# Query and key halves leave the projection stage, stacked scores of a differential attention, transposes between the score halves

## The reference

```python
def diff_attn_block(q1, q2, k1, k2, v, lam):
    scale = B_HEAD_DIM ** -0.5
    s1 = jnp.einsum('bhqd,bhkd->bhqk', q1, k1).astype(jnp.float32) * scale
    s2 = jnp.einsum('bhqd,bhkd->bhqk', q2, k2).astype(jnp.float32) * scale
    p = jax.nn.softmax(s1, axis=-1) - lam * jax.nn.softmax(s2, axis=-1)
    return jnp.einsum('bhqk,bhkd->bhqd', p.astype(v.dtype), v)
...
    p = h @ w_in                         # 2 x 512 columns for the convolution, 512 q, 512 k, 512 v
    qx = rope_2d(qx)                     # only the 1024 tokens are rotated, not the context
    kx = rope_2d(kx)
    u = a[..., :A_WIDTH] * jax.nn.sigmoid(a[..., A_WIDTH:])
    u = depthwise_conv(u, conv_w, conv_b)      # 31 taps
```

## Time and profile before

| | |
|---|---|
| median of 3 runs | 4222.05 us (4220.51 to 4226.47) |
| the profiled execution, its own time | 4207.65 us |
| its span (first to last instruction) | 4206.0 us |
| mean granted clock of TensorE | 0.92 |
| TensorE busy | 3500.0 us (83%) |
| VectorE busy | 2124.1 us (51%) |
| ScalarE busy | 1261.2 us (30%) |
| GpSimd busy | 223.8 us (5%) |

### The profile page before, as it was taken

How to read it: one execution, slowest core, us unless ns; L and a number is a source line. 1 busy time by engine, 2 the same in 40 slices (tenths; PEclk the granted TensorE clock), 3 DMA queues, 4 the chain that set the end, 5 groups by cost and what they waited for, 6 DMA issues and landing times. The chain is left out here.

```text
span 4206.0 us, 48006 instructions
## 1 busy us (share of the span) xinstructions
PE 3500.0 (83%) x18199; PEld 2870.6 (68%) x18199; DVE 2124.1 (51%) x2406; ACT 1261.2 (30%) x2015; POOL 223.8 (5%) x335
## 2 busy tenths in 40 slices
PE   2898677739799999999494888888888479999996
PEld 1776455527688888888393767667776468888884
DVE  4598354474434434444452565555556454444445
ACT  2111244353211112111242554444455222111121
POOL 0011000001100000000030000000000010000000
PEclk6899788879899999999696999999999789999998
DMA  4211433223211011100322000000000521111112
GB/s 158 68 60 62 165 136 133 91 90 120 61 40 50 30 35 35 50 30 21 136 87 76 14 12 12 12 12 4 13 5 6 185 81 47 47 56 40 50 50 90
DMA packets 233242, 259.87 MB, mean 62 GB/s; under 512 B 51424, under 2 KB 190400, under 8 KB 232112
## 3 DMA queue, kind: packets, MB, share of 16 engines
q1 hardware_dynamic: 226768, 241.02, 17.6%
q0 software_dynamic: 6368, 17.39, 1.3%
HBM read 217.42 MB, written 40.96 MB: 61 GB/s over the span
## 5 line engine op out<-in xcount | busy, mean ns | idle before, releaser
L1010 DVE TENSOR_TENSOR y_sum<-ffn_down_ps,y_sum 128x512 f32<-128x512 f32 x396 | 271.7, 690 | 253.1 <-PE ffn_down_ps L90 253.1
L88 PE MATMUL ffn_gate_ps<-y_hi,ffn_w_hi 128*128 128x512 f32 (+1 forms) x880 | 326.0, 370 | 31.8 <-DVE ffn_w_lo L971 31.8
L89 PE MATMUL ffn_gate_ps<-y_lo,ffn_w_hi 128*128 128x512 f32 (+1 forms) x880 | 325.5, 370 | 0.0
L90 PE MATMUL ffn_gate_ps<-y_hi,ffn_w_lo 128*128 128x512 f32 (+1 forms) x880 | 325.1, 369 | 0.0
L89 PE MATMUL ffn_val_ps<-y_lo,ffn_w_hi 128*128 128x512 f32 (+1 forms) x880 | 323.9, 368 | 0.0
L88 PE MATMUL ffn_val_ps<-y_hi,ffn_w_hi 128*128 128x512 f32 (+1 forms) x880 | 323.8, 368 | 0.0
L90 PE MATMUL ffn_val_ps<-y_hi,ffn_w_lo 128*128 128x512 f32 (+1 forms) x880 | 323.7, 368 | 0.0
L88 PE MATMUL ffn_down_ps<-ffn_w_hi,ffn_act_hi 128*128 128x512 f32 x792 | 312.1, 394 | 13.2 <-DVE y_sum L1010 6.8
L89 PE MATMUL ffn_down_ps<-ffn_w_lo,ffn_act_hi 128*128 128x512 f32 x792 | 309.6, 391 | 0.0
L90 PE MATMUL ffn_down_ps<-ffn_w_hi,ffn_act_lo 128*128 128x512 f32 x792 | 309.3, 390 | 0.0
L971 DVE TENSOR_TENSOR ffn_w_lo<-ffn_raw,ffn_w_hi 128x1024 fp32r<-128x1024 f32 x132 | 158.0, 1223 | 280.9 <-ACT ffn_w_hi L934 280.9
(11 more groups left out here) (270 smaller groups left out, 7764.6 us busy)
## 6 DMA issues: line engine op xcount, KB each, us to landing
ffn_raw<-in_ffn_w_up SPq DMA_DIRECT2D x88, 512.0 KB, 3.8
da_ada_w<-in_ada_w SPq DMA_DIRECT2D x10, 4096.0 KB, 13.0
ffn_raw<-in_ffn_w_down SPq DMA_DIRECT2D x44, 512.0 KB, 5.6
ab_raw<-in_ab_w_in SPq DMA_DIRECT2D x20, 512.0 KB, 3.7
scratch_x<-out_x SPq DMA_DIRECT2D x18, 512.0 KB, 2.6
mod_ada_w<-in_ada_w SPq DMA_DIRECT2D x4, 2048.0 KB, 11.1
scratch_qk<-ab_qk POOLq DMA_DIRECT2D x8, 640.0 KB, 3.3
da_raw<-scratch_qk SPq DMA_DIRECT2D x8, 640.0 KB, 4.7
```

Source lines behind the costliest of these rows:

```text
L88: pe.matmul(out, a_hi, b_hi, start=first, stop=False)
L89: pe.matmul(out, a_hi, b_lo, start=False, stop=False)
L90: return pe.matmul(out, a_lo, b_hi, start=False, stop=last)
L1010: dve.tensor_tensor(part, down_ps[:, half, :], part, ALU.add).then_inc(s.sum_done, 1)
```

## The change

Four things change.

1. In the projection stage GpSimd splits each finished q or k piece: a cast to fp32r (`qk_hi`), a subtraction (`qk_lo`), and two stores to two DRAM tensors.
2. The attention stage loads the parts. `q_stacked` holds on partitions 0 to 63 the hi part of q and on 64 to 127 the lo part, with the two score halves side by side in the free dimension; `k_hi` and `k_lo` are loaded twice, once on each half of the partitions. Six loads per head take the place of two, and no engine splits.
3. A score half is then two matmuls per chunk, stacked q by `k_hi` and stacked q by `k_lo`, over 128 rows each (with them the product lo by lo is computed as well). The first half's scores wait for the first exponential only, the second half's for the second.
4. The queues: TensorE puts the groups of transposes between the two halves' scores; products come one unit later; the modulation group moves to n % 4 == 2; VectorE runs combine(n) ahead of maxima(n+1).

```diff
@@ GpSimd, projection stage
                 for j in range(2):
                     n = i * 2 + j
                     pool.wait_ge(s.sum_done.sem, s.sum_done.nth(n))
-                    pool.dma_start(qk[n * P:(n + 1) * P, :], qk_t[:, j, :]).then_inc(qk_stored[j].sem, 16)
-                for j in range(2):
-                    pool.wait_ge(qk_stored[j].sem, qk_stored[j].nth(i))
-                    pool.sem_inc(s.qk_free.sem, 1)
+                    if i:
+                        pool.wait_ge(qk_stored[j].sem, qk_stored[j].nth(i - 1))
+                    pool.tensor_copy(qk_hi[:, j, :], qk_t[:, j, :]).then_inc(s.qk_hi_done.sem, 1)
+                    pool.wait_ge(s.qk_hi_done.sem, s.qk_hi_done.nth(n))
+                    if n:
+                        pool.wait_ge(qk_stored[1 - j].sem, qk_stored[1 - j].nth((n - 1) // 2))
+                    pool.tensor_tensor(qk_lo[:, :], qk_t[:, j, :], qk_hi[:, j, :].bitcast(F32), ALU.subtract)\
+                        .then_inc(s.qk_free.sem, 1)
+                    pool.dma_start(qk[0][n * P:(n + 1) * P, :], qk_hi[:, j, :].bitcast(F32)).then_inc(qk_stored[j].sem, 16)
+                    pool.wait_ge(s.qk_free.sem, s.qk_free.nth(n))
+                    pool.dma_start(qk[1][n * P:(n + 1) * P, :], qk_lo[:, :].bitcast(F32)).then_inc(qk_stored[j].sem, 16)
@@ SyncE, attention stage
+            def head(h):
+                j, rows = h % 2, B_HEADS * 2 * B_DIM
+                if h >= 2:
+                    sp.wait_ge(s.s2_full.sem, (h - 1) * NU)
+                def halves(part, first):
+                    return qk[part][first + h * 2 * B_DIM:first + (h + 1) * 2 * B_DIM, :]\
+                        .rearrange("(a d) t -> d a t", a=2)
+                for part in range(2):
+                    at = slice(part * B_DIM, (part + 1) * B_DIM)
+                    sp.dma_start(q_st[at, j, :, :].bitcast(F32), halves(part, 0)).then_inc(qk_in[j].sem, 16)
+                for k, part in ((k_hi, 0), (k_lo, 1)):
+                    for copy in range(2):
+                        sp.dma_start(k[copy * B_DIM:(copy + 1) * B_DIM, j, :, :].bitcast(F32), halves(part, rows))\
+                          .then_inc(qk_in[j].sem, 16)
@@ VectorE
-            for n in range(ALL + 2):
+            for n in range(ALL + QP + 1):
+                if n < ALL:
+                    combine(n)
                 if n + 1 < ALL:
                     maxima(n + 1)
-                if n % QP == 1 and n > QP:
-                    output(n // QP - 1)
+                if n and pair_at(n - 1) is not None:
+                    output(pair_at(n - 1))
                 if n and window(n - 1) is not None:
                     m.add(dve, window(n - 1))
-                if n < ALL:
-                    combine(n)
-                    if split_at(n):
-                        second_half(*split_at(n))
@@ TensorE
-            def scores(n):
+            def scores(n, half):
...
-                    for q, k in ((q_hi, k_hi), (q_lo, k_hi), (q_hi, k_lo)):
-                        for half, full in ((0, s.s1_full), (1, s.s2_full)):
-                            dims = slice(half * B_DIM, (half + 1) * B_DIM)
-                            mm = pe.matmul(s_ps[:, half, keys], q[dims, j, rows], k[dims, j, keys],
-                                           start=q is q_hi and k is k_hi, stop=k is k_lo)
-                            if k is k_lo and a + width == T:
-                                mm.then_inc(full.sem, 1)
+                    pe.matmul(s_ps[:, half, keys], q, k_hi[:, j, half, keys], start=True, stop=False)
+                    mm = pe.matmul(s_ps[:, half, keys], q, k_lo[:, j, half, keys], start=False, stop=True)
+                mm.then_inc(full.sem, 1)
...
-            for n in range(ALL + 1):
-                if n + 2 < ALL:
-                    scores(n + 2)
-                if n < ALL:
-                    turned(n)
-                if n % QP == 0 and n:
-                    product(n // QP - 1)
+            for n in range(ALL + QP):
+                for at in range(3):
+                    if n < ALL and at < len(groups(n)):
+                        turned(n, at)
+                    if n + 2 < ALL and at < 2:
+                        scores(n + 2, at)
+                if pair_at(n) is not None:
+                    product(pair_at(n))
                 if window(n) is not None:
```

More of the change, by code:

```diff
@@ L529, in project_conv_diff @@
         part = sb("part", [P, 2, SEQ])
+        qk_hi = sb("qk_hi", [P, 2, T], F32R)
+        qk_lo = sb("qk_lo", [P, T], F32R)
         v_t = sig
@@ L1186, in _ @@
             m.load(sp, 0)
-            piece(1, 0)
-            piece(1, 1)
+            head(1)
+            m.load(sp, 1)
             values(1)
-            m.load(sp, 1)
             m.load(sp, 2)
-            piece(2, 0)
-            piece(2, 1)
+            head(2)
             m.load(sp, 3)
@@ L1196, in _ @@
             m.load(sp, 4)
-            piece(3, 0)
-            piece(3, 1)
+            head(3)
             m.load(sp, 5)
```

97 lines of the change are left out of this document (39 added, 58 removed).

## The result

The changed kernel takes 4153.74 us (median of 4, 4149.86 to 4158.33). The kernel before took 4221.28 us beside it (median of 4, 4214.8 to 4226.47). The ratio is 0.9841, 95% interval 0.9824 to 0.9858: faster by 1.6%. The forecast was 4180 with a range of 4132 to 4214; the gain was forecast at 42 us and came out at 67.5.

A forecast was written before the change was run, and what follows sets the result against it. The prediction took attention to be bound by waits in a ring between engines and projection by VectorE. Attention -83, projection +36 and start +5 gave -42, from the median 4222.05 to 4180 us, range 4132 to 4214 (forecast's own case 4155 to 4205).

The forecast's parts named there:

- the rival without exclusion: Projection stage: GpSimd's casts and subtractions run beside VectorE's convolution, losing only 8 us; 4152 us, chance 0.12.
- Attention, -83 forecast: Attention stage: four heads of 66 us plus 8 for the start and 7.5 for the tail, 280 us, 83 less.
- my 7% on top of the walk: Attention heads: queue walk gave 62 us, raised to 66 because the old ring's walk fell some 7% short of the trace.
- The ring of 6.35 us: Attention, plain unit: combine, first maximum to first exponential, second exponential, and its becoming visible follow one another, about 6.35 us.
- a clock near 1: Attention stage: TensorE's longest idle gap falls from 4.04 to 2.5 us, so its granted clock rises from 0.84 to near 1.
- The splits explain about 40 us: Attention stage before: without splits a head costs about 77 us and the stage about 323, so splits explain 40 of 363.
- Projection, +36 forecast: Projection stage: GpSimd's operations cost 28.5 us in turns 1 to 3 and 7 for the last pieces; bounds 27 and 45.
- The exclusion: Projection stage: GpSimd and VectorE block each other, so each GpSimd cast (2.0 us) or subtraction (2.75) costs VectorE its whole length.
- Start, +5 forecast: Start of attention: 3.9 MB in six loads before the first scores; +0 at 410 GB/s, +9 at half rate, middle taken.
- The clock that stays low: Attention stage: TensorE's clock keeps 0.84, a head takes 74 us and the stage 311; 4211 us, chance 0.11.
- Only the splits' gain: Attention wins only the splits' 40 us and the projection stage gives them back; 4223 us, chance 0.07.
- The wait for the output: Attention: second transposes wait for VectorE's output, closing a ring of 9.7 us per product unit; at worst 4239 us, chance 0.08.

The follow-up runs named there:

- one_product: Changed kernel without the score matmuls with k's rest (q times k_lo left out); ratio 0.9827 to the kernel before, attention stage 258.1 us.
- split_moved_only: Kernel before with only the split moved to the projection stage, attention unstacked and in its old order, loading parts; 4222.56 us against 4217.85.
- The 2x2 table: Stacked kernels with TensorE's and VectorE's orders each old or changed; stage: both old 339.1, VectorE's changed 320.2, TensorE's changed 367.0, both 269.6 us.
- no_pool_split: Changed kernel without GpSimd's cast and subtraction of q and k in the projection stage, the unsplit sum stored twice; 4130.54 us.
- maxima_first: Changed kernel with VectorE doing maxima(n+1), output and the ada addition ahead of combine(n), as before; 4254.31 us.

## Why the prediction was right, and where it was off

**The sign and its cause** were right: attention wins far more than projection and start lose. At the end of attention the balance was -60.7, forecast -42. The number 4153.74 itself proves little: it lies just below the forecast's own 4155 to 4205 and beside the 4152 of the rival without exclusion, which the traces refute. Attention won 16.9 us more than forecast, projection lost 5.0 less and the start 3.3 more.

**Attention, -83 forecast, -99.9 measured.** Of the 16.9 us between them, 6.6 were a reading error: I took the output at 829.66 for the last, and the stage before was that much longer. The other 10 are in the stage after, 269.6 instead of 280. The heads came every 64.0, 64.6 and 65.2 us (first maxima at 508.55, 572.50, 637.08 and 702.30), the last with its tail took 73.2, against 66 and 73.5: my 7% on top of the walk was too much. The start took 2.6 us from first scores to first maxima, not the 8 that I allowed. The ring of 6.35 us a plain unit was right: five maxima in a row begin 6.36 us apart (515.18 to 540.62). So was a clock near 1 (0.98), but not its reason, the shorter gaps: in one_product TensorE's longest wait for an exponential was 2.3 us, about the 2.2 of the changed kernel, and its clock was 0.89.

**What carried it was put wrongly.** "The splits explain about 40 us" is a mis-sized term: moving them alone is worth 26.5. The misread output is in it as well. From the maxima at 745.32 to the true last output the fourth head takes 90.9 us, not 84.3; with my 7.5 for the tail a head without splits is then 83.4, the stage 349, and the splits explain some 20. In split_moved_only the heads take 85.1, 83.8 and 80.0 us, not 77. Against that, the order is worth 69.5 where the forecast left some 43 for it. I wrote that what the halves buy is the ring, with `combine` in it as an added 1.9 us. The 2x2 table shows that without `combine` in front TensorE's new queue buys nothing and costs 27.9, since its first transposes stand ahead of the scores and wait for `combine`. VectorE's moved lines were no price of the new order but its condition.

**Stacking** was priced at +18 us of TensorE's time, and the pitch of 0.23 us for a single matmul is as forecast (538.49 to 538.72). In the old order it cost the stage nothing (343.0 to 339.1): TensorE was busy for 273.4 us instead of 269.9, at a clock of 0.91 instead of 0.87. Its price came at the start: 12.1 us, of which the moved split gives 3.7 back. In one_product, in the new order, 39 us less of matmuls gave 11.5.

**Projection, +36 forecast, +31.0 measured.** The exclusion was right in kind: no_pool_split shows that the convolution's longer steps are GpSimd's doing. The cast was mis-sized, 1.25 to 1.40 us instead of 2.0. The subtraction takes 2.88 undisturbed; the forecast had worked out 2.9 and added up 2.75. That each operation costs VectorE its whole length was a little too much: two of each are 8.3 us, and a turn grew by 6.7. One of the two casts falls on the rotation, whose addition took 2.17 instead of 1.23, a loss of 0.9. So the three turns cost 22.0 us instead of 28.5 (the third store of the convolution went from 348.15 to 370.10), and the last pieces 9.0 instead of 7: the two errors partly cancel. GpSimd's subtraction did wait for the store before it, four times and 14.0 us in all, which the forecast put under the cast; what that costs was not separated.

**Start, +5 forecast, +8.3 measured.** I took the middle of two bounds, +0 and +9; the upper one, loads at half the rate, was right.

**Rivals.** No exclusion: refuted by the steps beside GpSimd. The clock that stays low: refuted at 0.98. Only the splits' gain: refuted by the 69.5 us of the order; split_moved_only, which has the splits' gain alone, comes out level as said. The wait for the output: it exists on VectorE (45.9 us) and ScalarE (26.9 us), but TensorE waits for no output ahead of its second transposes, and the ring of 9.7 us did not close. In maxima_first a ring of 10.5 us did, through product, output and `combine`.

## What to carry to other kernels

When two engines hand work back and forth, change both queues together and test each alone: half of a good reordering can be slower than none (367.0 against 339.1), and the whole much better than either. In a stage where an engine waits for another's last result, look for work that is already free to run and put it between the halves of the waiting operation. Work that is moved to an idle engine is not free if it takes the bound engine's access with it: GpSimd's casts and subtractions cost VectorE 6.7 us a turn, while its own subtractions cost 3.0.

## What the runs showed of the hardware

- GpSimd's cast f32 to fp32r over 128x1280 takes 1.25 us undisturbed, its subtraction 2.88, VectorE's 1.48. Three-operand convolution steps of VectorE (1.57 us) reach 4.26 us beside GpSimd; with its casts and subtractions left out all 120 stay at 1.56 to 1.57.
- Loads that fill 64 partitions each ran at 205 GB/s, the same bytes over 128 partitions at 324 with the start of the transfers included.
- With loads whose source begins with a dimension of 2, the DMA engines were busy for 0.12 to 0.13 of the time. The third to sixth such load stood some 12 us each in SyncE's queue, and so did the load of lambda behind them; the first two took 0.6.
- With 208 of 1768 matmuls left out, TensorE's granted clock in the stage fell from 0.98 to 0.89, and its busy time by 18.7 us where 39 had been left out.
